# First norms turned to token partitions, short loads on SyncE's queue, gate rank in four column tiles, its logs under k and v, modulation slabs spread out

## The chip, the cores and the metric

One core of a Trainium2 chip runs the kernel. The time is device microseconds of one execution, and comparisons use the median of several. The profile is one execution. TensorE is PE in the rows (PEld its weight loads), VectorE DVE, ScalarE ACT, GpSimd POOL, SyncE SP. A q behind an engine's name is its instruction queue issuing a DMA.

## The reference

A transformer stack on 256 tokens of width 1024. The first block, cut to what matters:

```
sh1, sc1, g1, sh2, sc2, g2      = split(silu(c) @ w_mod + b_mod)        # x
csh1, csc1, ...                 = split(silu(c_ctx) @ w_mod + b_mod)    # context
hc = rmsnorm(ctx, norm1_g) * (1 + csc1) + csh1
hx = rmsnorm(x,   norm1_g) * (1 + sc1)  + sh1
u, q, k, v, g, gates, lr = split(h @ w_in)      # lr: 2 x 16 columns, "gate rank"
la_f = log_sigmoid(lr_f @ a2_f + ab_f) / 16     # the same for b; for hx and hc
pooled = centred_pool(ux) - ux
o = gla_bidirectional(qx, kx, vx, la_x, state from kc, vc, la_c)
x = x + g1 * mixer_out(pooled, o, g, gates)     # sigmoid gates, w_pool_br, w_gla_br, w_o
x = x + g2 * hier_moe(rmsnorm(x, norm2_g) * (1 + sc2) + sh2)   # 32 experts
```

Behind it come a final norm and a second block: two layers (block attention, dilated attention), each with a layer norm and an MLP of width 4096 with squared relu. The change touches the first block up to `w_o` only.

## The kernel before

**Slabs.** Weights come in slabs of 2 MB. `slab_plan()` lists them; SyncE issues them in that order (the loop over `SLAB_AT`, `load`, L592). Up to the experts a slab's number modulo 4 is its slot, so a slab can be issued only when the slab four places ahead of it in the list has been read (`slab_freed`). `w_mod` is slabs mod 0 to 11 (512 columns each); mod 0 and 1 are the shift of the first norm, 2 and 3 its scale, 4 to 11 the rows g1, sh2, sc2, g2. `w_in` slab 0 is u, 1 q, 2 k, 3 and 4 v, 5 and 6 g, 7 to 10 the gates.

**Banks.** `bank_plan()` lists every PSUM result in order with the engine that reads it out (V: VectorE, A: ScalarE). A ring of 4 banks is used in that order; `bank()` on TensorE waits until the result four places back was read out. `moved(engine, name, i)` waits for one read-out. A second PSUM area, `acc`, holds sums of w_o and later.

**Order of the work.** Each engine has one program. On TensorE: ctx and x tiles are turned so that features lie on partitions (`turn`, L1625); the small vectors are turned (L1674); for each of the two norms eight matmuls with a ones matrix sum the squares over features (`norm_sum`, L1737); four modulation row products (`mod_rows`, L1685: column tiles of 32, so four partial sums over two steps), whose rows are copied by ScalarE (L719) and turned to columns by tiny matmuls (`mod_cols`, L1692); VectorE then forms hT and cT (`affine`, L1082). The gate rank `lr` (L1754) is one 16-column product at a time for direction and stream, copied by ScalarE to `lrT` (L762); the gate product `z` (L1762) adds the bias by a 17th row of ones. ScalarE takes the absolute value (L767), exp (L769) and ln (L770), VectorE min (L1101) and the difference (L1107), which gives L, the log decay. Then cumulative sums and remainders of L (L1770, L1775, L1782, L1784) with exp on ScalarE, k for x and context (`fmajor` L1632, `tmajor` L1639), ktok, v (eight products of 32 records), q, the four heads (L1817 to L1844), u, pooling (L1857) and y1 (L1865).

After that come the exact products: `f_half` takes half a slab, split into a high part by ScalarE (`split_hi`, L735) and a low part by VectorE (`split_lo`, L1031), two halves ahead (`WB`), and makes three matmuls per block (L1644 to L1646). Between these halves stand `mod_rows(4)` to `mod_rows(11)` and the broadcasts of their rows over all partitions (`mod_bc`, L1697), the slabs taking turns in `slab_plan()`. Then the `w_o` sums (L1710 to L1712), and everything behind.

**Small loads.** ScalarE's queue issues ten short loads after x has landed (`small`, L694): the rank weights (rows of 128 B), pool weights, router weights (rows of 16 and 128 B), the gate matrices and biases. One semaphore counts all ten. SyncE issues identity, ctx, x, six vector rows, the other constants and then slabs.

## Time and profile before

| | us |
|---|---|
| time before, median of 3 (lowest to highest) | 1555.63 (1553.88 to 1557.14) |
| the profiled execution's own time | 1555.18 |
| its span | 1553.4 |
| TensorE matmul busy in the span | 1396.1 |
| VectorE busy | 652.8 |
| ScalarE busy | 467.8 |
| DMA, mean over the span | 239 GB/s |

The span runs from the first to the last instruction; times of day in the rows count from its start. Mean granted TensorE clock: 0.956 of full speed. Some rows are of one long line of work, some group many instructions.

### The profile page before, as it was taken

Reading aid. Unit: us, or ns where it says so; the run is one execution under the profiler, and the core shown is the slowest. Engines: PE = TensorE matmul, PEld = TensorE weight load, DVE = VectorE, ACT = ScalarE, POOL = GpSimd, SP = SyncE. Lnnn points to the kernel's source line nnn. Section 1 sums busy time; section 2 is a strip of 40 time slices with the busy share of each in tenths; the row PEclk is TensorE's granted clock in tenths of the full one; section 3 lists DMA queues with packets and bytes.
Section 4 is the critical chain, followed back from the end, with each engine's and each line's share of the span. In section 5 each row is a group of like instructions: output and inputs, shape, how many; then the busy total and the mean of one; then the engine's idle time right before and its main releaser. Section 6 shows DMA issues by size and latency. Waiting matters only on the chain.

```text
span 1553.4 us, 20788 instructions
## 1 busy us (share of the span) xinstructions
PE 1396.1 (90%) x8683; PEld 1005.6 (65%) x8683; DVE 652.8 (42%) x968; ACT 467.8 (30%) x598; POOL 0.2 (0%) x4
## 2 busy tenths in 40 slices
PE   3889998999969998888888969997999989799998
PEld 2445464787854443443443439987999879689997
DVE  1322033333552331231222336657555576565555
ACT  1260112341331221111111134544333345443332
POOL 0000000000000000000000000000000000000000
PEclk6889999999969999999999989998999999989999
DMA  9601221876648999999999995243554525345430
GB/s 320 217 1 54 84 106 54 310 274 247 227 163 367 427 430 427 430 427 430 427 429 428 428 405 200 106 165 121 198 217 170 209 90 182 124 163 185 155 148 27
DMA packets 88678, 371.77 MB, mean 239 GB/s; under 512 B 6356, under 2 KB 8194, under 8 KB 76196
## 3 DMA queue, kind: packets, MB, share of 16 engines
q1 hardware_dynamic: 84604, 369.40, 60.6%
q10 hardware_dynamic: 4008, 1.40, 0.4%
q8 instruction: 52, 0.85, 0.2%
q14 instruction: 14, 0.11, 0.0%
HBM read 369.74 MB, written 1.05 MB: 239 GB/s over the span
## 4 chain that ended last, share of the span: by engine, by line
PE 67%; DMA 19%; DVE 6%; ACT 5%; issue 2%; ACTq 1%; DVEq 0%; SPq 0%
DMA arena<-in_moe_w 18%; PE ring L1644 6%; PE ring L1645 6%; PE ring L1646 6%; PE ring L1639 5%; PE acc L1710 4%; PE acc L1711 4%; PE acc L1712 4%; PE ring L1966 4%; PE acc L1991 3%; PE ring L1632 3%; PE ring L1981 2%; PE acc L1644 2%; PE acc L1646 1%; PE acc L1645 1%
## 5 line engine op out<-in xcount | busy, mean ns | idle before, releaser
L859 ACT ACTIVATE arena<-ring 128x512 f32<-128x512 f32 x80 | 52.9, 661 | 382.7 <-PE ring L1966 230.0
L1031 DVE TENSOR_TENSOR wlo<-slots,whi 128x2048 fp32r<-128x2048 f32 x56 | 128.0, 2288 | 73.6 <-ACT whi L735 73.6
L1348 DVE COPY arena<-ring 128x512 f32<-128x512 f32 x48 | 44.5, 927 | 240.9 <-PE ring L1966 213.0
L735 ACT ACTIVATE whi<-slots 128x2048 fp32r<-128x2048 f32 x56 | 106.9, 1913 | 97.5 <-PE acc L1712 62.4
L1991 PE MATMUL acc<-arena 128*128 128x512 f32 x256 | 118.4, 605 | 0.0
L1966 PE MATMUL ring<-slots,arena 128*32 128x512 f32 x768 | 94.0, 618 | 13.0 <-DMA slots<-in_moe_w 13.0
L1991 PEld LDWEIGHTS acc<-arena 128*128 128x128 f32 x256 | 46.1, 190 | 73.3 <-issue 45.8
L1646 PE MATMUL ring<-xhi,wlo 128*128 128x256 f32 x320 | 90.7, 283 | 0.0
L1645 PE MATMUL ring<-xlo,whi 128*128 128x256 f32 x320 | 90.7, 283 | 0.0
L1644 PE MATMUL ring<-xhi,whi 128*128 128x256 f32 x320 | 90.6, 283 | 0.0
L1973 PEld LDWEIGHTS ring<-const,arena 128*128 128x128 f32 x512 | 63.4, 196 | 38.4 <-issue 16.7
L1031 DVE TENSOR_TENSOR w1lo<-slots,w1hi 128x2048 fp32r<-128x2048 f32 x20 | 45.8, 2292 | 89.5 <-ACT w1hi L735 89.5
L1639 PE MATMUL ring<-slots,arena 128*128 128x512 f32 x192 | 83.0, 593 | 0.0
L1973 PE MATMUL ring<-const,arena 128*128 128x128 f32 x512 | 75.0, 292 | 2.8 <-DVE arena L1348 0.6
L1644 PE MATMUL acc<-xhi,whi 128*128 128x256 f32 x224 | 67.7, 302 | 3.5 <-DVE xlo L1390 3.5
L1966 PEld LDWEIGHTS ring<-slots,arena 128*32 128x32 f32 x768 | 21.5, 111 | 73.6 <-issue 53.7
L1710 PE MATMUL acc<-whi,hidhi 128*128 128x512 f32 x176 | 69.1, 392 | 0.0
L1711 PE MATMUL acc<-wlo,hidhi 128*128 128x512 f32 x176 | 68.8, 391 | 0.0
L1712 PE MATMUL acc<-whi,hidlo 128*128 128x512 f32 x176 | 68.5, 389 | 0.0
L1639 PEld LDWEIGHTS ring<-slots,arena 128*128 128x128 f32 x192 | 36.4, 190 | 44.8 <-issue 44.8
L1646 PE MATMUL acc<-xhi,wlo 128*128 128x256 f32 x224 | 64.9, 290 | 0.0
L1645 PE MATMUL acc<-xlo,whi 128*128 128x256 f32 x224 | 64.7, 289 | 0.0
(317 smaller groups left out, 2976.0 us busy)
## 6 DMA issues: line engine op xcount, KB each, us to landing
slots<-in_moe_w SPq DMA_DIRECT2D x64, 2048.0 KB, 24.6
arena<-in_moe_w SPq DMA_DIRECT2D x32, 2048.0 KB, 27.2
slots<-in_mlp_w_in SPq DMA_DIRECT2D x16, 2048.0 KB, 9.2
slots<-in_mlp_w_out SPq DMA_DIRECT2D x16, 2048.0 KB, 7.7
slots<-in_w_mod SPq DMA_DIRECT2D x12, 2048.0 KB, 8.6
slots<-in_w_in SPq DMA_DIRECT2D x11, 2048.0 KB, 12.2
slots<-in_moba_w_qkv SPq DMA_DIRECT2D x6, 2048.0 KB, 20.1
slots<-in_dil_w_qkv SPq DMA_DIRECT2D x4, 2048.0 KB, 8.0
```

Of the source, the lines that this page charges most:

```text
L735: act.activation(hi, raw, ACT.Copy).then_inc(G["whi_ready"], 1)
L1031: dve.tensor_tensor(lo, raw, hi.bitcast(F32), ALU.subtract).then_inc(G["split_ready"], 1)
L1639: ins = pe.matmul(b[:, 0:n], x[:, kt, tt * P:(tt + 1) * P], w[:, kt, 0:n], start=(kt == 0), stop=(kt == ks - 1))
L1644: pe.matmul(o, whi_, xhi_, start=first, stop=False, skip_group_check=True)
L1645: pe.matmul(o, whi_, xlo_, start=False, stop=False, skip_group_check=True)
L1646: return pe.matmul(o, wlo_, xhi_, start=False, stop=last, skip_group_check=True)
L1710: pe.matmul(o, hi[:, k0 + k, t_], wh[:, k, c], start=(first and k == 0), stop=False, skip_group_check=True)
L1711: pe.matmul(o, hi[:, k0 + k, t_], wl[:, k, c], start=False, stop=False, skip_group_check=True)
L1712: ins = pe.matmul(o, lo[:, k0 + k, t_], wh[:, k, c], start=False, stop=(last and k == ks - 1), skip_group_check=True)
L1966: ins = pe.matmul(b[32 * g:32 * g + 32, :], xs[:, kt, j, :], w[:, kt, :], start=(kt < 4), stop=(kt >= 4))
L1973: ins = pe.matmul(b[:, f * P:(f + 1) * P], src[:, f * P:(f + 1) * P], C("fold"), start=True, stop=True)
L1991: ins = pe.matmul(acc[:, tt, f], putT[:, j, tt * P:(tt + 1) * P], ys[:, f], start=False, stop=True, skip_group_check=True)
```

## The change

The norms of ctx and x are taken with tokens on partitions: ScalarE squares a token tile and sums along the row, takes one root for each pair, VectorE scales the rows, and then the tiles are turned. Scale and shift follow in two halves of features, x on VectorE, context on ScalarE. The modulation slabs come in the order 0, 2, 1, 3. Vector rows move to ScalarE's queue; the ten short loads move to SyncE's, at four places of the slab list, with three semaphores in place of one; the gate matrices are loaded twice, to partitions 0, 32, 64 and 96. The rank's four products go to four column tiles of one bank. The gate's eight products read partitions 0, 32, 64, 96 and go to four ring banks and four banks of `acc`; exp and ln are each done for both halves in a row. The k products of x, two v products and modulation slab 4 stand between the gate and the cumulative sums. Modulation slabs 4 to 8 stand among v and q, 9 and 10 in the heads, 11 at u. `w_in` 5 to 10 follow all modulation slabs in the list. All four bias rows are broadcast at once when hT is complete.

```diff
+MODS = (0, 2, 1, 3)
 def slab_plan():
-    order = [("mod", s) for s in range(4)]
-    order += [("w_in", 2), ("w_in", 3), ("w_in", 4), ("w_in", 1), ("w_in", 0)]
-    order += [("mod", 4), ("w_in", 5), ("mod", 5), ("w_in", 6), ("mod", 6)]
-    for s in range(4):
-        order += [("w_in", 7 + s), ("mod", 7 + s)]
-    order += [("pool_br", 0), ("mod", 11), ("gla_br", 0), ("gla_br", 1), ("w_o", 0), ("w_o", 1)]
+    order = [("mod", s) for s in MODS]
+    order += [("w_in", 2), ("w_in", 3), ("mod", 4), ("mod", 5), ("w_in", 4), ("mod", 6), ("w_in", 1), ("mod", 7)]
+    order += [("mod", 8), ("w_in", 0), ("mod", 9), ("mod", 10), ("mod", 11)]
+    order += [("w_in", s) for s in range(5, 11)]
+    order += [("pool_br", 0), ("gla_br", 0), ("gla_br", 1), ("w_o", 0), ("w_o", 1)]
     order += [("moe", s) for s in range(3 * NE)]
     for l in range(2):
...
-                if (name, s) == ("w_in", 5):
-                    sp.wait_ge(G["h_ready"], 2 * KT)
-                    spread(bc_g1, a["b_mod"][0][2 * D:3 * D], bc_in)
-                    spread(bc_sh2, a["b_mod"][0][3 * D:4 * D], bc_in)
+                if (name, s) == ("w_in", 2):
+                    sp.dma_start(w_lr[:, :, :], a["w_in"][0][:, 5632:5664].rearrange("(k p) n -> p k n", p=P)).then_inc(lr_in, 16)
+                    for j in range(4):
+                        d = "fb"[j % 2]
+                        sp.dma_start(a2[32 * j:32 * j + RANK, :], a["gla_a2_" + d][0]).then_inc(lr_in, 16)
+                        sp.dma_start(a2[32 * j + RANK:32 * j + RANK + 1, :], a["gla_ab_" + d]).then_inc(lr_in, 16)
+                if (name, s) == ("w_in", 3):
+                    sp.dma_start(const[:, P + 2:], a["consts"][:, P + 2:]).then_inc(consts_in, 16)
+                if (name, s) == ("mod", 4):
+                    sp.wait_ge(G["h_ready"], KT)
+                    for j, dst in enumerate((bc_g1, bc_sh2, bc_gain2, bc_g2)):
+                        spread(dst, a["b_mod"][0][(2 + j) * D:(3 + j) * D], bc_in)
+                if (name, s) == ("mod", 6):
+                    sp.dma_start(w_pool[:, :, :], a["pool_w"][0].rearrange("g c e -> c g e")).then_inc(pool_in, 16)
+                if (name, s) == ("w_in", 0):
+                    sp.dma_start(w_rt[:, :, 0:NG], a["router_grp_w"][0].rearrange("(k p) n -> p k n", p=P)).then_inc(router_in, 16)
+                    sp.dma_start(w_rt[:, :, NG:], a["router_exp_w"][0].rearrange("(k p) n -> p k n", p=P)).then_inc(router_in, 16)
+                    sp.dma_start(rb[0:1, 0:NG], a["router_grp_b"]).then_inc(router_in, 16)
+                    sp.dma_start(rb[0:1, NG:], a["router_exp_b"]).then_inc(router_in, 16)
                 if (name, s) == ("gla_br", 1):
                     sp.wait_ge(bank_full, BANK_AT["gate", 7] + 1)
...
-            act.wait_ge(tokens_in["x"], 16)
-            small(w_lr[:, :, :], a["w_in"][0][:, 5632:5664].rearrange("(k p) n -> p k n", p=P))
-            small(w_pool[:, :, :], a["pool_w"][0].rearrange("g c e -> c g e"))
-            small(w_rt[:, :, 0:NG], a["router_grp_w"][0].rearrange("(k p) n -> p k n", p=P))
-            small(w_rt[:, :, NG:], a["router_exp_w"][0].rearrange("(k p) n -> p k n", p=P))
-            for d, name in enumerate("fb"):
-                small(a2[0:RANK, d, :], a["gla_a2_" + name][0])
-                small(a2[RANK:RANK + 1, d, :], a["gla_ab_" + name])
-            small(rb[0:1, 0:NG], a["router_grp_b"])
-            small(rb[0:1, NG:], a["router_exp_b"])
...
-                mod_rows(s)
+            act.wait_ge(G["eps_ready"], 1)
+            for n, (src, name) in enumerate(((ctok, "ctx"), (xtok, "x"))):
+                act.wait_ge(tokens_in[name], 16)
+                for tt in range(TT):
+                    i = TT * n + tt
+                    act.activation(squares[i], src[:, tt, :], ACT.Square, accum_out=nss[:, i:i + 1]).then_inc(G["square_ready"], 1)
+                act.wait_ge(G["square_ready"], TT * n + TT)
+                pair = slice(TT * n, TT * n + TT)
+                act.activation(nstd[:, pair], nss[:, pair], ACT.Sqrt, bias=oeps[:, 0:1], scale=1.0 / D).then_inc(G["nstd_ready"], 1)
+            for i in range(4):
+                tt, q = divmod(i, 2)
+                b = take("c_tiles", i).rearrange("p (k t) -> p k t", k=4)
+                act.activation(cT[:, 4 * q:4 * q + 4, tt * P:(tt + 1) * P], b, ACT.Copy).then_inc(freed["A"], 1)
+            def c_affine(q):
+                act.wait_ge(G["mod_ready"], q + 1)
+                for kt in range(4 * q, 4 * q + 4):
+                    act.activation(cT[:, kt, :], cT[:, kt, :], ACT.Identity, bias=mod[:, kt, 1:2], scale=scale1[:, 1, kt:kt + 1]).then_inc(G["c_ready"], 1)
+            moved(act, "c_tiles", 3)
+            mod_rows(0)
+            mod_rows(2)
+            mod_rows(1)
+            c_affine(0)
+            mod_rows(3)
+            c_affine(1)
+            b = take("lr", 0)
             act.wait_ge(G["lr_ones"], 1)
-            for i in range(2):
-                b = take("lr", i)
-                ins = act.activation(lrT[0:RANK, 2 * i:2 * i + 2, :], b[0:RANK, :].rearrange("p (d t) -> p d t", d=2), ACT.Copy)
-                ins.then_inc(freed["A"], 1)
+            for j in (2, 3):
+                p_ = slice(32 * j, 32 * j + RANK)
+                act.activation(lrT[p_, :], b[p_, 0:T], ACT.Copy).then_inc(G["lr_part"], 1)
+            for tt in range(TT):
+                for j in range(4):
+                    if tt == 0:
...
+                if i == 0:
+                    mod_rows(11)
                 split_hi(i)
             for i in range(4):
-                if i % 2 == 0:
-                    mod_rows(4 + i // 2)
                 b = take("g", i)
                 split_hi(i + WB)
                 ins = act.activation(gT[:, 2 * i:2 * i + 2, :], b.rearrange("p (k t) -> p k t", k=2), ACT.Silu)
...
+            for n, src in enumerate((ctok, xtok)):
+                dve.wait_ge(G["nstd_ready"], n + 1)
+                pair = slice(TT * n, TT * n + TT)
+                link(dve.reciprocal(nstd[:, pair], nstd[:, pair]))
+                for tt in range(TT):
+                    dve.tensor_scalar(src[:, tt, :], src[:, tt, :], nstd[:, TT * n + tt:TT * n + tt + 1], None, ALU.mult).then_inc(G["tn_ready"], 1)
+            for i in range(4):
+                tt, q = divmod(i, 2)
+                b = take("x_tiles", i).rearrange("p (k t) -> p k t", k=4)
+                dve.tensor_copy(xT[:, 4 * q:4 * q + 4, tt * P:(tt + 1) * P], b).then_inc(freed["V"], 1)
+            for q in range(2):
+                mod_cols(q)
+                mod_cols(2 + q)
+                moved(dve, "mod_cols", 2 + q)
+                v = slice(4 * q, 4 * q + 4)
+                for r in range(2):
+                    ins = dve.scalar_tensor_tensor(scale1[:, r, v], mod[:, KT + 4 * q:KT + 4 * q + 4, r], 1.0, col("norm1_g", 4 * q, 4), ALU.add, ALU.mult)
+                ins.then_inc(G["mod_ready"], 1)
+                moved(dve, "x_tiles", 3)
+                dve.wait_ge(G["mod_ready"], q + 1)
+                for kt in range(4 * q, 4 * q + 4):
+                    dve.tensor_scalar(hT[:, kt, :], xT[:, kt, :], scale1[:, 0, kt:kt + 1], mod[:, kt, 0:1], ALU.mult, ALU.add).then_inc(G["h_ready"], 1)
+            b = take("lr", 0)
+            for j in range(2):
+                p_ = slice(32 * j, 32 * j + RANK)
+                if j == 1:
+                    dve.wait_ge(G["lr_part"], 2)
+                ins = dve.tensor_copy(lrT[p_, :], b[p_, 0:T])
+            ins.then_inc(freed["V"], 1)
+            for tt in range(TT):
+                for j in range(4):
+                    dve.wait_ge(G["abs_ready"], 4 * tt + j + 1)
+                    dve.tensor_scalar(L[:, 2 * j + tt, :], z_bank(j, tt), 0.0, None, ALU.min).then_inc(freed["V"] if tt == 0 else v_step, 1)
+                    n_step[0] += tt
+            for i in range(2):
+                ins = dve.tensor_copy(kT[:, 2 * i:2 * i + 2, :], take("kT", i).rearrange("p (h t) -> p h t", h=2))
...
+            split_lo(0)
+            mod_bc(11)
+            split_lo(1)
             for i in range(2):
                 ins = dve.tensor_copy(pooled[:, 2 * i:2 * i + 2, :], take("pool", i).rearrange("p (g t) -> p g t", g=2))
...
-            def norm_sum(name, k, src):
-                b = bank(name, k)
-                for kt in range(KT):
-                    ins = pe.matmul(b[:, 0:T], ones, src[:, kt, :], start=(kt == 0), stop=(kt == KT - 1))
-                full(ins)
-            for k in range(2):
-                pe.wait_ge(G["sq_ready"], k + 1)
-                norm_sum("norm", k, sq)
-            for s in range(4):
+            for n, s in enumerate(MODS):
                 mod_rows(s)
-                if s:
...
+            mod_cols(MODS[-1])
+            pe.wait_ge(lr_in, 16 * 9)
+            b = bank("lr", 0)
+            for kt in range(KT):
+                pe.wait_ge(G["h_ready"], kt + 1)
+                pe.wait_ge(G["c_ready"], kt + 1)
+                for j in range(4):
+                    d = j % 2
+                    ins = pe.matmul(b[32 * j:32 * j + RANK, 0:T], w_lr[:, kt, d * RANK:(d + 1) * RANK], (hT, cT)[j // 2][:, kt, :],
+                                    start=(kt == 0), stop=(kt == KT - 1))
+            full(ins)
+            moved(pe, "lr", 0)
+            for tt in range(TT):
+                for j in range(4):
+                    p_ = slice(32 * j, 32 * j + RANK + 1)
+                    o = bank("z", j) if tt == 0 else z_bank(j, tt)
+                    pe.matmul(o, lrT[p_, tt * P:(tt + 1) * P], a2[p_, :], start=True, stop=True).then_inc(bank_full if tt == 0 else G["z2_ready"], 1)
+            wk = arrive("w_in", 2, KT, 512)
+            for i in range(2):
+                full(fmajor(bank("kT", i), wk, hT, 2 * i * P, 2))
+            mod_rows(4)
+            def values_x_or_c(i):
+                s, j = divmod(i, 4)
+                w = arrive("w_in", 3 + s, KT, 512)
+                full(tmajor(bank("v", i), w, (hT, cT)[j // 2], j % 2))
+            values_x_or_c(0)
+            pe.wait_ge(consts_in, 16)
+            mod_bc(4)
+            values_x_or_c(1)
             for i in range(4):
                 d, hp = divmod(i, 2)
                 pe.wait_ge(G["L_ready"], d + 1)
...
                                             S[:, d, n, :], start=False, stop=(d == 1), skip_group_check=True)
                 full(ins)
+                if h > 1:
+                    mod_bc(h + 7)
+                if 0 < h < 3:
+                    mod_rows(h + 8)
             w = arrive("w_in", 0, KT, 512)
-            for i in range(2):
-                ins = tmajor(bank("u", i), w, hT, i)
-                full(ins)
+            full(tmajor(bank("u", 0), w, hT, 0))
+            mod_rows(11)
+            full(tmajor(bank("u", 1), w, hT, 1))
+            mod_bc(11)
             moved(pe, "u", 1)
             for i in range(2):
                 b = bank("pool", i)
```

## Rows read from the trace of the kernel before

**Rows 1.** Chain of waits, 340 to 441 us: start, length, what ran or was awaited.
```profile
341.39 0.86 PE ring L1697 x2
...
365.23 0.59 ACT arena L819
...
414.13 0.47 PE acc L1710
```

**Rows 2.** Chain of waits, 0 to 110 us.
```profile
1.65 7.27 DMA arena<-in_x
...
13.26 6.54 ACTq L694
...
19.83 5.84 ACTq L694
...
58.66 1.89 PE ring L1692 x16
...
61.62 15.67 PE ring L1754 x64
...
95.20 1.91 ACT arena L770
```

**Rows 3.** Groups by shape on TensorE, 0 to 260 us: count, busy us, mean ns, idle.
```profile
L1754 PE MATMUL ring<-arena 128*16 128x256 f32 x64 | 15.7, 411 | 1.1 <-DVE arena L1082 1.1
...
L1685 PE MATMUL ring<-slots,arena 128*32 128x512 f32 x64 | 7.5, 597 | 0.0
```

**Rows 4.** Windows: length, busy by engine, then clock, DMA share, GB/s.
```profile
15.00:30.00 15.00, 0.31 (x1) 0.18 (x1) 0.07 (x1) 2.44 (x4) 0.00 (x0) 0.50 1.10 354
...
55.00:60.00 5.00, 5.00 (x45) 2.79 (x37) 0.88 (x4) 1.19 (x2) 0.00 (x0) 1.00 1.05 397
...
82.90:96.60 13.70, 8.15 (x24) 4.93 (x23) 4.93 (x7) 13.60 (x12) 0.00 (x0) 0.51 0.00 1
...
270.00:274.00 4.00, 4.00 (x21) 1.32 (x19) 1.75 (x4) 0.00 (x0) 0.00 (x0) 0.57 0.07 22
...
434.50:455.00 20.50, 16.01 (x57) 12.80 (x58) 9.06 (x27) 8.69 (x11) 0.00 (x0) 0.51 0.44 187
```

**Rows 5.** Groups by shape on ScalarE, 0 to 260 us.
```profile
L767 ACT ACTIVATE arena<-ring 128x512 f32<-128x512 f32 x8 | 4.4, 595 | 2.0 <-PE ring L1762 2.0
...
L769 ACT ACTIVATE arena<-arena 128x2048 f32<-128x2048 f32 x2 | 3.8, 1910 | 0.0
...
L802 ACT ACTIVATE arena<-arena 128x256 f32<-128x256 f32 x8 | 3.3, 416 | 0.2
...
L769 ACT ACT_TABLE_LOAD x2 | 2.6, 1283 | 0.0
```

**Rows 6.** Chain of waits, 0 to 340 us, its part from 108 us.
```profile
108.78 13.81 PE ring L1632 x64
...
137.20 54.93 PE ring L1639 x128
...
207.53 1.97 PE ring L1817 x8
...
249.08 13.95 PE ring L1639 x32
```

**Rows 7.** DMAs: ScalarE's queue, 0 to 400 us; landing of w_in slabs, 0 to 350.
```profile
q10 hardware_dynamic: 3720, 0.61, 1.0%
...
DMA to landing us min/median/max: 7.9/12.2/18.2
```

**Rows 8.** Timeline in order of time, 249 to 310 us.
```profile
263.04 0.37 SPq L592 DMA_DIRECT2D slots<-in_w_in  x1
...
265.47 2.29 DVE L1031 TENSOR_TENSOR w1lo<-slots,w1hi 128x2048 fp32r<-128x2048 f32 x1 [4.58 <-ACT w1hi L735]
...
269.01 2.55 PE L1865 MATMUL ring<-arena 128*128 128x256 f32 x8 [3.27 <-DVE arena L1169]
...
274.43 0.38 PE L1644 MATMUL ring<-hhi,w1hi 128*128 128x256 f32 x1
```

More of the change, by code:

```diff
@@ L269, in build @@
         sq = at(20 * K1, KT, T)
+        squares = [at(o * K1, D) for o in (20, 21, 24, 25)]
         cT = at(22 * K1, KT, T)
@@ L1130, in _ @@
                 ins.then_inc(freed["V"], 1)
+            for s in range(5, 8):
+                mod_bc(s)
             for i in range(2):
@@ L1696, in mod_bc @@
                 moved(pe, "mod_rows", s)
-                full(pe.matmul(bank("mod_bc", s), C("selb"), mod_row[:, s % 2, :], start=True, stop=True))
+                full(pe.matmul(bank("mod_bc", s), C("selb"), mod_slot(s), start=True, stop=True))
             def t_half(h, hi, lo, k0, first, last, f0, tiles=(0, 1), ready=None):
@@ L1757, in _ @@
-            moved(pe, "lr", 1)
-            for i in range(8):
-                st, tt = divmod(i, 2)
-                d = st % 2
-                b = bank("z", i)
-                full(pe.matmul(b, lrT[:, st, tt * P:(tt + 1) * P], a2[:, d, :], start=True, stop=True))
+            for n, s in enumerate(MODS):
+                mod_rows(s)
+                if n:
+                    mod_cols(MODS[n - 1])
+            mod_cols(MODS[-1])
+            pe.wait_ge(lr_in, 16 * 9)
+            b = bank("lr", 0)
@@ L1785, in _ @@
                 full(ins)
-            w = arrive("w_in", 2, KT, 512)
             for i in range(2):
-                full(fmajor(bank("kT", i), w, hT, 2 * i * P, 2))
-            for i in range(2):
-                ins = tmajor(bank("kc", i), w, cT, i)
-                full(ins)
+                full(tmajor(bank("kc", i), wk, cT, i))
             moved(pe, "kT", 1)
@@ L1877, in _ @@
                 turn("oT", i, otok, *divmod(i, 2))
[L1878 to L1885 removed]
+            for i in range(8):
+                f_half(bank("gate", i), 4 + i, hhi, hlo)
             w = arrive("pool_br", 0, POOLG, D)
```

293 lines of the change are left out of this document (109 added, 184 removed).

## Prediction

> **What bounds the kernel now.** I read the chain of waits first, then windows of busy time with the granted clock, then groups by shape on TensorE and ScalarE, then the SyncE issues. From 0 to the first sum matmul of w_o at 414.1 us [rows 1] the chain is never held by the slab stream as a whole: it is a string of waits on one core's program order. From there on (experts, both attention layers, both MLPs, about 1139 us) the change touches no instruction, and the expert stage starts from the end of w_o; so whatever w_o gains or loses I carry to the end one for one.
>
> Before 414 us there are four places to see. (1) Up to 60.6 us, where the last modulation columns end [rows 2]: x lands at 8.9, then ScalarE's queue issues ten short loads until 27.5, two of them holding it 6.54 and 5.84 us, and both norms run one after the other through TensorE. (2) 61.6 to 77.3: the gate rank, 15.67 us of TensorE on 16 columns [rows 2, 3]. (3) 77.3 to 99.6: gate and its logs; from 82.9 to 96.6 ScalarE works 13.6 of 13.7 us while TensorE's clock is granted at 0.51 [rows 4], that is mostly the 1.2 GHz level. (4) From 271 to 414 TensorE is full, with eight modulation slabs between the large products.
>
> **The change part by part.** Each step gets its new time of day; durations are those of before.
>
> *Start.* The slabs of modulation 0, 2, 1, 3 now set the pace. Ahead of the last of them lie the identity and pair columns, ctx, x and four slabs: 0.07 + 2.10 + 8.39 = 10.55 MB. With the short loads beside them the DMAs moved 354 GB/s, without them 397 [rows 4]. I take 380 and 2.5 us before bytes flow: 30.3 us (354 to 397 gives 29.1 to 32.3). The norms are ready before that: the rows load on ScalarE's queue, two pairs of squares, two roots and four scalings by row (1 to 1.3 us each at these lengths), and eight transposed tiles, end near 23 even if half of them run at the low clock. Then row product 3 (1.87 us, a fourth of the group at L1685 [rows 3]), its copy behind four context affines on ScalarE (0.42 us each [rows 5]), column products 1 and 3: 34.6 us where it was 60.6. Gain 26.
>
> *Gate rank.* 32 matmuls of 256 columns now go to four column tiles. L1685 is the row for that: 16 records of 512 columns in 1.87 us, 0.117 each, where a 512-column record alone takes 0.43 (13.81 us for 64 of half that length [rows 6]). So 64 records of 256 columns take 64 x 0.058 = 3.7 us. Bounds: 3.7, and 15.7 if the tiles did not overlap. I take 3.7, since L1685 has the same K, type and tile width. End 38.3. The copies are now two on ScalarE and, after them, the last on VectorE, 1.4 us instead of 0.6: 39.7.
>
> *Gate.* Eight matmuls with 17 rows, now at partitions 0, 32, 64, 96. No row of before shows four row tiles at once; one after the other they take two 0.43 us records each (6.9 in all), overlapped four deep two rounds of 0.86 and a start, 1.9. The Trainium skill, TensorEngine Tiling (Array Packing), Performance Considerations, says a contract dimension up to 32 tiles fourfold; by it 1.9, and no row here shows that. I take 1.9 because the bank destinations are separate, and keep 6.9: 41.6 us. The two kT products (13.8 [rows 6]) then run beside the logs. The logs need 8 x 0.55 + 4 x 1.91 + 2 x 1.28 = 14.6 us [rows 5] (two table loads instead of four), so they end near 55, and four subtractions of 1.2 us on VectorE near 59; nobody waits, since the cumulative sums come at 73. This cover is worth the 19 us of logs and waits between 77.9 and 97.1 [rows 2].
>
> *Modulation 4 arrives late.* SyncE waits for all of hT (36.5 us), then issues four broadcasts of bias rows (2.1 MB) and slab 4. From 30.3 the queue holds the short rows, w_in 2, the constants 1.25 MB, w_in 3, the broadcasts, slab 4: 9.6 MB at 380 is 25.3 us, plus the short rows. ScalarE's queue moved 3720 packets in 1.0% of 400 us [rows 7], so 1100 packets cost 1.2 us: slab 4 is in at 57. kT ends at 55.4; TensorE waits 1.6 us. This wait also swallows the first 1.6 us of any slower gate or rank.
> The Trainium skill, DMA: Bandwidth & Descriptors, Specifications, speaks against the move: transfers under 512 B per row fall off line rate. Our rank weights are 128 B rows and stand in front of w_in 2 in one queue; the row on the 3720 packets says this costs about a microsecond.
>
> *k, v, q with modulation 4 to 8.* Row product 4, v0, broadcast 4 (0.86 [rows 1]), v1: 57 to 73.5. Sums and remainders 12.2 (14.4 in the trace, part of it at the low clock), kc 13.7, ktok 0.9: 100.3. Then six v tiles (54.93 for eight [rows 6]) 41.2, qT 13.8, four row products 7.4, four broadcasts 3.4. Slab 6 is freed only by v3, slab 8 by v7; each has one product (6.9 and 7.8) in front of it against the shortest landing of 7.9 [rows 7]: 1.1 + 0.3 us. Heads start at 168.2; they started at 207.5.
>
> *Heads and u.* 41.5 us as before [rows 6], plus row products 9, 10 and 11 (5.6), broadcasts 9 and 10 (1.7) and 1 us for their handovers, plus u (13.9): u ends at 232.0 (before 263.0).
>
> *A new wait.* w_in 5 sat in its slot 60 us early; now its slot is the one u reads, so it is issued at the end of u and lands 7.9 us later. ScalarE's order is split 0, then the copy of u1; TensorE's pooling waits for that copy. Chain: landing 7.9, split 1.9, copy 0.6; pooling 2.0 while ScalarE splits 1; VectorE low half 0, broadcast 11, low half 1, pooled copies (2.3 + 0.7 + 2.3 + 1.3): 16.5; y1 2.6: first gate matmul at u + 19.2 = 251.2. Before it was at u + 11.4, with 2.9 of row product 4 inside [rows 8]. During the wait of 10 us TensorE's clock falls (0.57 after a lesser one [rows 4]); I add 2.5 us of half speed in pooling and the first g half.
>
> *Large products.* 274.4 to 414.1 [rows 1, 8] less seven row products (13.0), eight broadcasts (6.9), and the 1.7 us that ypool waited for a gate [rows 1] behind the late gla_br slab: 139.7 - 21.6 = 118.1. w_o starts at 251.2 + 2.5 + 118.1 = 371.8, before 414.1: 42.3 us earlier. The splits (1.9 and 2.3 us for each half) stay under the 5.8 us of a half.
>
> The profiled execution took 1555.2 us (span 1553.4 and 1.8 around it), 0.4 below the median. 1555.2 - 42.3 = 1512.9; I say **1513 us**.
>
> **Rivals.**
> *Tiles don't overlap.* Rank +12.0, gate +5.0, less the 1.6 us that slab 4 swallows: 1513 + 15.4 = 1528 with both, 1516.4 with the gate alone. For: no row tiles in the trace. Against: L1685.
> *Short rows clog SyncE.* Each of the rank's weight loads as slow as the two that held ScalarE's queue, 6.54 + 5.84: 12.4 us before lr and w_in 2, 1525. For: the queue did stall there. Against: those stalls happened with the engines full of slabs (354 GB/s went on flowing), so they are back pressure.
> *The clock stays low after the new wait.* From 434.5 to 455 it stayed at 0.51 for 20.5 us though TensorE was busy 16.0 of them [rows 4]. The same after u: 20 us at half speed give back 10 instead of 2.5: 1520.5. Against: there the matmuls were small and halting.
> *The new wait is shorter than I think, or the early phase finishes sooner* (slab 4 on time, faster slabs): 3 to 8 us better, 1507.
> *Slower than before.* One mechanism: TensorE stays at 1.2 GHz from the gate through v, q and heads because it never gets going. From 57 to 232 it has about 150 us of matmuls that run at the high clock in the trace; at half speed they double, 150 us more, 1663. It decides from 42 us of matmul at the low clock on. Against: after each pause in the trace the high clock came back within some 7 us of dense matmuls, and v is dense.
>
> **How the numbers follow.** Forecast 62%, with a range of its own of 1507 to 1519; tiles 10% (most of it the gate alone), clog 6%, clock after u 10%, better than forecast 8%, slower 2%; 2% for no change at all, in case a stage behind w_o takes back all. The range 1504 to 1526 takes in the likeliest, the clock, the clog and the better case and the lesser tile case. A measurement of this kernel tells 0.2% (3.1 us) from nothing. Faster 0.96, same 0.02, slower 0.02.
>
> **What would show it.** In the new profile: last modulation column near 34.6; the rank group four times shorter; gate records short or 0.86 apart; TensorE dense from 42 us but for a gap near 55; heads from 168; u ending at 232; then a gap of about 10 us on TensorE with w_in 5 landing inside it; no row products after 235; w_o from 372. Wrong if slab 3 lands after 33, if v or q wait on slabs for more than 3 us in all, or if the gap behind u is over 15.

## The result, and the profile after

The changed kernel takes **1520.4 us** (median of four runs, 1519.04 to 1522.69). The kernel before took 1555.47 us beside it (four runs, 1553.88 to 1557.14). The ratio is 0.9776, with a 95% interval of 0.9759 to 0.9793: faster by 35 us. The forecast was 1513 us, so it is 7.4 us too low: inside the whole range of 1504 to 1526, but 1.4 us outside the range of 1507 to 1519 that the likeliest case had for itself. The profiled execution took 1521.46 us, with a span of 1519.7 us at a granted clock of 0.960 (before 0.956).

The chain of waits of the changed kernel, 0 to 441 us (start, length, what ran or was awaited):

```profile
10.78 21.47 DMA slots<-in_w_mod
...
32.30 3.37 PE ring L1696 x16
...
37.54 3.62 PE ring L1757 x64
...
45.09 15.74 PE ring L1646 x64
...
77.47 3.57 PE ring L1788 x32
...
121.05 8.02 DMA slots<-in_w_mod
...
154.77 8.43 DMA slots<-in_w_mod
...
237.25 7.93 DMA slots<-in_w_in
...
245.21 1.92 ACT w1hi L733
...
247.15 2.29 DVE w1lo L1053
...
249.44 0.60 DVE arena L1079
250.04 2.20 DVE w1lo L1053
252.24 1.21 DVE arena L1192 x2
253.49 3.77 PE ring L1893 x8
...
378.96 0.47 PE acc L1721
```

Read it beside [rows 1, 2, 6]. The start is now one long wait for a modulation slab (10.78 to 32.30). The rank group is 3.62 us long, where it was 15.67. No ScalarE log stands in the chain between the gate and the sums. The big gap of before between the last modulation column and k has gone, and a new one has opened at 237.25: from the end of u to the first gate matmul at 257.3, TensorE's order hangs on the landing of w_in 5 and then on five short steps of ScalarE and VectorE. On this chain w_o comes in at 378.96 instead of 414.13, 35.2 us earlier. These are the sum matmuls that wait for the last part of their input; the first ones, which the prediction took 414.1 for, ran at 406.62 before and run at 371.02 now, 35.6 us earlier. Behind 378.96 the span has 1140.7 us left, where it had 1139.3 behind 414.13.

Windows of the changed kernel (length, busy by engine, clock, DMA share, GB/s):

```profile
3.00:28.00 25.00, 13.24 (x97) 8.79 (x97) 6.02 (x12) 11.60 (x20) 0.00 (x0) 1.00 1.04 388
28.00:32.00 4.00, 0.25 (x3) 0.16 (x2) 1.78 (x7) 2.07 (x4) 0.00 (x0) 0.98 1.12 303
32.00:37.00 5.00, 4.71 (x29) 2.00 (x29) 0.17 (x1) 0.60 (x1) 0.00 (x0) 0.67 1.05 379
46.00:50.00 4.00, 4.00 (x13) 3.21 (x13) 3.12 (x6) 3.97 (x6) 0.00 (x0) 0.64 1.03 406
237.00:257.30 20.30, 8.67 (x29) 6.77 (x28) 7.17 (x7) 4.19 (x3) 0.00 (x0) 0.66 0.87 311
257.30:271.00 13.70, 13.70 (x116) 13.70 (x115) 3.33 (x4) 5.90 (x5) 0.00 (x0) 1.00 0.93 329
```

Two things are to be seen. In the last four microseconds before slab 3 is in, TensorE is idle and the DMAs move 303 GB/s, not 388. And around the pauses of TensorE the clock falls: it is granted at half from 31.9 to 35.3 us, that is from just before the end of the wait for slab 3, and again from 45.5 to 48.9 us and inside the new gap, so that the windows there show about 0.65. Once the gate's products run dense it is 1.00 again.

Groups by shape on TensorE, 0 to 260 us, of the changed kernel:

```profile
L1765 PE MATMUL ring<-arena 17*128 17x512 f32 x8 | 1.1, 640 | 1.3 <-DVE arena L1110 1.3
L1765 PE MATMUL acc<-arena 17*128 17x512 f32 x8 | 1.0, 587 | 0.0
```

Sixteen gate records with a mean of about 600 ns are done in 2.1 us of busy time: they lie four deep over each other. In the trace they start in fours, at 42.5, 43.0, 43.4 and 43.9 us.

### The profile page after: what moved, and what is told of

Its sections match the earlier page's. It is cut to its first block, busy times and chain, and to the rows that moved or that the text cites. A ratio compares the mean times of both kernels' runs of the same rounds, so it can differ in the third digit from the quotient of the medians.

```text
span 1519.7 us, 20742 instructions
## 1 busy us (share of the span) xinstructions
PE 1372.5 (90%) x8651; PEld 994.1 (65%) x8651; DVE 645.3 (42%) x966; ACT 467.0 (31%) x608; POOL 0.2 (0%) x4
## 4 chain that ended last, share of the span: by engine, by line
PE 66%; DMA 21%; DVE 6%; ACT 4%; issue 2%; SPq 1%; DVEq 0%; ACTq 0%
DMA arena<-in_moe_w 18%; PE ring L1658 6%; PE ring L1659 6%; PE ring L1660 6%; PE ring L1653 5%; PE acc L1721 4%; PE acc L1722 4%; PE acc L1723 4%; PE ring L1979 4%; PE acc L2004 3%; DMA slots<-in_w_mod 2%; PE ring L1646 2%; PE ring L1994 2%; PE acc L1658 2%; PE acc L1659 2%
## 5 line engine op out<-in xcount | busy, mean ns | idle before, releaser
L733 ACT ACTIVATE w1hi<-slots 128x2048 fp32r<-128x2048 f32 x20 | 38.2, 1910 | 91.3 <-PE ring L1660 71.2
```

What stands on the lines that cost most here:

```text
L733: act.activation(hi, raw, ACT.Copy).then_inc(G["whi_ready"], 1)
```

## Experiments

The first six undo or repair one part each, the next three go into the start, the last are combinations. All ratios are against the kernel before, and "w_o" is the time of the first sum matmul of w_o in the profiled execution, which is 371.02 us in the changed kernel. Of the expectations, the one on the slabs that are not spread (365 and 379) counts w_o on the chain of waits, 8 us later; the others that name 371, 363, 357 or 354 count it as here.

### The gap behind u: copies before the low halves

```diff
@@ ScalarE, end of u
                 if i == 0:
                     mod_rows(11)
+            for i in range(2):
                 split_hi(i)
@@ VectorE
-            split_lo(0)
             mod_bc(11)
-            split_lo(1)
             ... pooled and y1 copies ...
+            split_lo(0)
+            split_lo(1)
```

> The changed kernel, with the copy of u1 on ScalarE ahead of the first two high halves, and the pooling and y1 copies on VectorE ahead of the first two low halves. Theory (the gap behind u is one chain: landing of w_in 5 7.9, high half 1.9, and only then the copies that pooling and y1 wait for): pooling and y1 run while w_in 5 lands, the first gate matmul comes 12.2 us behind u instead of 20.0, and the time falls by 8 us to about 1512.5. Rival (the slab's landing alone makes the gap, so the order of copies is free): first gate matmul still 18 to 20 us behind u, time unchanged at 1520.4.

Measured 1517.49 us (1516.09 to 1520.11), ratio 0.9754 [0.9734, 0.9775]. Its chain of waits:

```profile
238.06 8.12 DMA slots<-in_w_in
...
246.21 1.92 ACT w1hi L733
...
248.15 2.30 DVE w1lo L1054
...
250.59 0.55 PE ring L1659
```

The gate's product starts 12.5 us after u instead of 20.0: the pooling chain has left the path and only landing, one high and one low half stand in it. So the gap is made as the prediction said, and 7.5 us of it are a matter of order. w_o starts 5.7 us earlier, but the median moved by only 2.9 us where 8 were expected. In the profiled execution the expert stage behind w_o took 460.7 us (419.85 to 880.56) instead of 458.1 (425.53 to 883.66); 1.6 us of that is longer TensorE time (411.21 instead of 409.64 us busy), at a mean clock of 0.97 instead of 0.98. That stage has no instruction of the edit in it, and no run shows why it differs.

### w_in 5 fetched before u

```diff
-    order += [("mod", 8), ("w_in", 0), ("mod", 9), ("mod", 10), ("mod", 11)]
-    order += [("w_in", s) for s in range(5, 11)]
+    order += [("mod", 8), ("w_in", 0), ("mod", 9), ("mod", 10), ("w_in", 5), ("mod", 11)]
+    order += [("w_in", s) for s in range(6, 11)]
...
-    order += [("u", 0, "A"), ("mod_rows", 11, "A"), ("u", 1, "A"), ("mod_bc", 11, "V")]
+    order += [("u", 0, "A"), ("u", 1, "A")]
...
+    order += [("g", 0, "A"), ("mod_rows", 11, "A"), ("g", 1, "A"), ("mod_bc", 11, "V"), ...]
```

> The changed kernel, with w_in 5 ahead of modulation 11 in the slab list, so that its slot comes free at q; row product and broadcast 11 behind the first and second g half. Theory (the gap behind u is made by the slot that w_in 5 shares with u's slab): no slab wait behind u, first gate matmul about 9 us behind u instead of 20.0, no low clock there, time about 1508 (12 us less). Rival (w_in 5 early collides with the loads of modulation 9 and 10 and of the heads, or modulation 11 is now late): the gap moves behind the first g half and the time falls by less than 4 us.

Measured 1513.12 us (1508.24 to 1515.57), ratio 0.9717 [0.9694, 0.9741], 7.3 us under the changed kernel, where 12 were expected. u ends at 238.27; its chain of waits goes on:

```profile
238.27 0.60 ACT arena L833
...
244.24 1.99 PE ring L1892 x8
```

No landing stands in it. The gate's product starts at 245.88, 7.6 us after u. w_o comes 8.0 us earlier, although in this execution the clock was low from 30.8 to 44.4 us and the early phase ended later for it.

### The modulation slabs where they were

The order of slabs, products and broadcasts 4 to 11 is put back as in the kernel before (slabs among w_in 5 to 10 and behind them, products between the gate's halves); everything else stays.

```diff
-    order += [("w_in", 2), ("w_in", 3), ("mod", 4), ("mod", 5), ("w_in", 4), ("mod", 6), ...]
+    order += [("w_in", 2), ("w_in", 3), ("w_in", 4), ("w_in", 1), ("w_in", 0)]
+    order += [("mod", 4), ("w_in", 5), ("mod", 5), ("w_in", 6), ("mod", 6)]
+    for s in range(4):
+        order += [("w_in", 7 + s), ("mod", 7 + s)]
```

> The changed kernel, with the slab list from w_in 2 on, and the row products and broadcasts of modulation 4 to 11, back where they were in the kernel before; everything else of the change stays. Theory (spreading them moves TensorE work without removing any, and its waits cost): the gap behind u shrinks from 20.0 to 11.4 us with row product 4 inside, the waits on slabs 6 and 8 (1.2 and 0.7 us), the handovers in the heads (1) and the wait of 3.3 us at the turned heads go, 1.7 us at ypool come back; w_o starts near 365 instead of 379, time 1506 to 1508. Rival (the spreading is part of the gain, since the large products no longer wait for slabs): w_o starts later than 379 and the time is 1522 to 1542.

Measured 1513.98 us (1509.23 to 1514.39), ratio 0.9733 [0.9717, 0.9749]: **6.4 us faster than the changed kernel**, though 6 us slower than expected. The profiled execution, the fastest of the four, has this in its chain of waits:

```profile
198.79 13.95 PE ring L1649 x32
...
213.35 1.81 ACT w1hi L734
...
222.50 2.83 PE ring L1692 x16
...
225.34 0.32 PE ring L1654
```

u ends at 212.75, the high half of w_in 5 is split straight away, and the gate's product follows 12.6 us after u, with a row product in it. The heads, too, start at 157.25 and not at 173.86, since four row products and their broadcasts no longer stand before them. w_o comes 12.2 us earlier in this execution; by the medians 6.4 us are left of it, and why the other executions are 4 to 5 us slower than this one is open. Moving the slabs was thus a loss of some 6 us inside a change that wins 35.

### The gate rank tile by tile

```diff
-            for kt in range(KT):
-                pe.wait_ge(G["h_ready"], kt + 1)
-                pe.wait_ge(G["c_ready"], kt + 1)
-                for j in range(4):
-                    d = j % 2
+            pe.wait_ge(G["h_ready"], KT)
+            pe.wait_ge(G["c_ready"], KT)
+            for j in range(4):
+                d = j % 2
+                for kt in range(KT):
```

> The changed kernel, with the rank's 32 matmuls ordered tile by tile (eight of one column tile in a row) instead of one of each tile in turn. Theory (the shortening comes from overlap of four neighbouring column tiles): the rank group takes about 14 to 15.7 us instead of 3.65, gate and all behind it 11 to 12 us later, time 1531 to 1532. Rival (the engine orders tiles by itself, or the shortening is from the 16-column form): the group stays near 4 us and the time at 1520.4.

Measured 1537.84 us (1534.45 to 1537.98), ratio 0.9879 [0.9859, 0.9899]: 17.4 us slower than the changed kernel. The chain of waits:

```profile
36.52 3.52 PE ring L1703 x16
...
42.75 14.07 PE ring L1757 x63
```

The windows of that group, these matmuls alone (TensorE, its weight loads, then clock, DMA share, GB/s):

```profile
42.75:48.15 5.40, 5.40 (x14) 1.86 (x16) 0.50 1.05 398
48.15:56.82 8.67, 8.66 (x52) 3.80 (x48) 1.00 1.04 394
```

The same 32 matmuls (64 records in the trace), into the same four column tiles, take 14.07 us when the eight of one tile follow each other, and 3.6 when neighbours go to different tiles. But the first 5.4 us of the 14.07 ran at half clock, and the 3.6 did not. Records of one tile start 0.427 us apart at the low clock and 0.216 us apart at the high one; only where one tile's row ends and the next begins do a few of them overlap. My estimate for the group at the high clock throughout is 14.07 - 2.7 = 11.4 us, so the order itself costs some 7.7 us. Of the 17.4 us the rest is the low clock in the group (2.7), my edit waiting for all features before its first matmul (2.7), and last columns that end 2.5 us later, since in this execution the clock was low from 31.1 to 48.1 us and slab 3 was used 0.6 us later. Some 2 us stay without a cause.

### The sums before k and v

The products of k, modulation 4 and the first two v tiles are moved behind the cumulative sums on TensorE, ScalarE and VectorE, so nothing covers the logs.

```diff
+            # cumulative sums and remainders here
             wk = arrive("w_in", 2, KT, 512)
             for i in range(2):
                 full(fmajor(bank("kT", i), wk, hT, 2 * i * P, 2))
             mod_rows(4)
             values_x_or_c(0)
             mod_bc(4)
             values_x_or_c(1)
-            # cumulative sums and remainders here
```

> The changed kernel, with k, row product 4, v0, v1 and broadcast 4 placed behind the cumulative sums again, so that nothing covers the logs. Theory (the cover is worth what the logs take on ScalarE less nothing): TensorE idles from 44.5 us until L of the first direction is ready near 57, 12.5 us, and 1 to 3 us of low clock follow; time 1533 to 1536. Rival (the wait for slab 4 and the later slab waits absorb the delay): slab 4's landing is reached in both, time 1520 to 1526.

Measured 1531.98 us (1531.74 to 1538.22), ratio 0.9847 [0.9831, 0.9864]: 11.6 us slower. The chain of waits, in the slowest of its executions:

```profile
48.54 4.01 ACT arena L777 x8
...
62.24 5.47 PE ring L1775 x32
```

TensorE waits from the gate's end at 49.9 to 62.24, 12.3 us, and the chain is ScalarE's absolute values, exp and ln with their table loads.

### Short loads back on ScalarE's queue

```diff
@@ SyncE, in front of w_in 2 (mod 6 and w_in 0: the pool and router loads)
-                    sp.dma_start(w_lr[:, :, :], a["w_in"][0][:, 5632:5664]...)
-                    for j in range(4):
-                        ... gla_a2, gla_ab ...
@@ ScalarE, before the norms
+            act.wait_ge(tokens_in["x"], 16)
+            act.dma_start(w_lr[:, :, :], a["w_in"][0][:, 5632:5664]...)
+            ... pool_w, router, gla_a2, gla_ab ...
```

> The changed kernel, with all the short loads back on ScalarE's queue behind the arrival of x (four pairs for the gate now, so 14 loads). Theory (their issue holds ScalarE some 18 us, with silu, squares and roots behind it): the norms' tiles come near 38 instead of 19.7, the last column near 46, time 1528 to 1531. Rival (the slabs are the bound and hide it): last column stays within 2 us of 37.5, time 1519 to 1522.

Measured 1536.09 us (1533.92 to 1537.08), ratio 0.9868 [0.9851, 0.9884]: 15.7 us slower. The chain of waits:

```profile
9.09 0.41 ACTq L705
...
12.90 6.63 ACTq L708
...
19.56 5.90 ACTq L711
...
34.83 5.84 PE ring L1639 x32
...
52.23 5.31 PE ring L1757 x64
```

ScalarE stands in the issues until 28.4 us, as in [rows 2], before it squares anything; the tiles are turned from 34.83 to 40.66 instead of 14.05 to 19.7, and the last column ends at 52.2 instead of 37.5. That is 6 us behind the expectation, and so the time is 5 us over it: the tiles are 2.7 us later than the 38 expected, and the four row products, their columns and ScalarE's context affines between them take 11.5 us behind the tiles, not 8. The two issues of 6.63 and 5.90 us are those of [rows 2] again, and in both cases the DMAs were full of slabs while they lasted, which fits back pressure on the issuing engine. They are the loads of router weights (rows of 128 B) and of the first gate matrix (16 rows of 2 KB). The rank weights, rows of 128 B too, were issued in 0.41 us (L705), so it is not the short rows that make an issue long. SyncE in the changed kernel, in order of time, says the same: the first gate matrix is issued in 3.75 us and its second copy in 0.31, and four slabs of 2 MB take 13.92.

```profile
2.16 13.92 SPq L605 DMA_DIRECT2D slots<-in_w_mod  x4
16.12 5.29 SPq L629 DMA_DIRECT2D arena<-in_w_in  x1
21.46 3.75 SPq L632 DMA_DIRECT2D arena<-in_gla_a_f  x1
...
27.79 0.31 SPq L632 DMA_DIRECT2D arena<-in_gla_a_f  x1
```

### Half of two slabs

Slabs 1 and 3 are fetched only by half; half of the sums of these two modulations are left out.

```diff
+                if SLABS[n] in (("mod", 1), ("mod", 3)):
+                    sp.dma_start(view(...)[:, 0:4, :], src[:, 0:4, :]).then_inc(landed[SLOT_OF[n]], 16)
+                    return
...
-                for half in range(2):
+                halves = 1 if s in (1, 3) else 2
+                for half in range(halves):
```

> The changed kernel, loading and using only the first half (features 0 to 511) of modulation slabs 1 and 3; the rest of their sums is left out. Theory (the landing of the fourth slab sets the start): slab 3 lands 5.4 us earlier, the last modulation column comes at 32 instead of 37.5, less 0.9 us more for each half product; time 1513 to 1515. Rival (the norms or the chain of tiles set the start): last column not before 36, time 1519 to 1521.

Measured 1514.55 us (1514.1 to 1517.23), ratio 0.9736 [0.972, 0.9753], 5.9 us faster. TensorE in order of time:

```profile
26.22 1.06 PE L1700 MATMUL ring<-slots,arena 128*32 128x512 f32 x8
...
29.41 1.87 PE L1707 MATMUL ring<-const,arena 128*128 128x2 f32 x8 [1.14 <-ACT arena L721]
```

The last column is done at 31.2 instead of 37.5 and w_o starts 6.4 us earlier: in the changed kernel the start is bound by the slabs' bytes, and what is won there reaches the end nearly one for one (6.3 us at the last column, 5.9 in the time). Here TensorE works without a pause from 19.7 to 28.3 us, so its own chain of products has become the bound; that still fewer bytes would win nothing more is argued from this and not shown.

### TensorE kept busy before slab 3

```diff
+                if n == 3:
+                    for _ in range(4):
+                        pe.matmul(acc[:, 0, 0:512], ident, xtok[:, 0, 0:512], start=True, stop=True)
```

> The changed kernel with four extra matmuls (512 columns, 3.4 us together, into an unused bank) on TensorE while it waits for modulation slab 3. Theory (the short wait drops the granted clock, and row product 3 and the first part of kT pay for it): row product 3 takes 1.9 instead of 3.4 us, kT 13.8 instead of 15.7, w_o starts 1.5 to 3.4 us earlier, time 1517 to 1519. Rival (the clock falls for another reason): row product 3 stays at 3.4 us, time 1520 to 1521.

The four matmuls write a bank that nobody reads then. Measured 1518.76 us (1517.56 to 1521.67), ratio 0.9763 [0.9747, 0.978]: 1.6 us under the changed kernel, within the intervals. TensorE in order of time:

```profile
31.73 1.92 PE L1696 MATMUL ring<-slots,arena 128*32 128x512 f32 x16
```

The row product takes 1.92 us instead of 3.37, so its length was the clock's doing. The columns end at 35.5. But the clock fell later, from 42.2 to 49.1 us, behind the pauses at rank and gate: part of what was won was given back in kT, and w_o starts 1.9 us earlier.

### Rank loads one slab later

```diff
-                if (name, s) == ("w_in", 2):
+                if (name, s) == ("w_in", 3):
                     sp.dma_start(w_lr[:, :, :], ...)
```

> The changed kernel, with the rank's nine loads issued behind w_in 2, before the constants, instead of in front of it. Theory (short rows run beside the last bytes of slab 3, where the DMAs moved 303 instead of 387 GB/s, and delay its landing by about 1 us): slab 3 is used at 31.3 instead of 32.3, but the rank then waits for its weights until about 39, so gate is 1 to 2 us later and the time 1520 to 1523. Rival (the short rows cost nothing, the start is bound by the slabs' bytes alone): row product 3 starts at 32.3 again.

Measured 1521.72 us (1520.28 to 1521.82), ratio 0.978 [0.9765, 0.9795]: no gain. One line of its windows, and two pieces of its chain of waits:

```profile
28.00:32.00 4.00, 0.47 (x7) 0.39 (x11) 1.78 (x7) 2.07 (x4) 0.00 (x0) 1.00 1.05 385
```

```profile
25.32 8.46 SPq L632
...
38.77 5.38 PE ring L1756 x64
```

Without the short rows the DMAs move 385 GB/s in the last four microseconds, not 303, but slab 3 is used only 0.45 us sooner (31.85). That is less than executions differ: the ten that have the short rows in front of w_in 2 and fetch slab 3 whole use it between 31.8 and 33.0 us. So this run can't say that they delay it at all. The issues themselves then become the wait: that of the first gate matrix, 16 rows of 2 KB, holds SyncE for 8.46 us, the last of the nine loads lands at 38.7, and the rank starts 1.2 us later than in the changed kernel, at the low clock.

### Combinations

Three kernels put the repairs together. The first is w_in 5 early with the four matmuls before slab 3. The second is the same with the turned heads behind the first gate half. The third is the old slab order with the four matmuls.

> As the run with w_in 5 early, plus four extra matmuls before row product 3. Theory (low clock at slab 3 costs it the 4 us by which its kT came later than in the changed kernel, 49.6 against 45.1): last column near 35.5, kT from 43, w_o near 357 instead of 363, time 1507 to 1511. Rival (no gain from the clock): 1513.

> The changed kernel with three edits together: w_in 5 ahead of modulation 11 (as in the run with w_in 5 early), four extra matmuls before row product 3, and the turned heads behind the first gate half. Theory (the three losses are separate: the slot behind u 9 to 12, the low clock at slab 3 2, the wait of 3.3 us at the turned heads): w_o starts near 354 where the changed kernel had 371, time 1503 to 1507, and TensorE has no wait over 1 us between the turned heads and the second gate half. Rival (the expert stage is bound by its own slab stream, whose start doesn't move with TensorE): time stays at 1512 to 1514 as with w_in 5 early alone.

> The run with the slabs not spread, plus the four extra matmuls before row product 3. Theory (where the modulation products stand is worth nothing by itself; only the slab waits are): it ties with the run that keeps them spread with w_in 5 early and the extra matmuls, 1506 to 1511, ratio 0.969 to 0.972. Rival (spread products are worth what they take out of the large products, once w_in 5 is early): 3 us or more slower than that run, 1511 or more.

| kernel | median us (range) | ratio [95%] |
|---|---|---|
| w_in 5 early, TensorE busy | 1508.21 (1506.96 to 1513.34) | 0.9707 [0.9689, 0.9724] |
| the same, turned heads later | 1508.05 (1504.31 to 1511.01) | 0.9695 [0.9679, 0.9711] |
| old slab order, TensorE busy | 1507.86 (1507.42 to 1509.1) | 0.9699 [0.9686, 0.9713] |

All three beat both kernels, by some 12 us the changed one, and can't be told from each other. The second has a new wait in its chain:

```profile
275.63 1.91 ACT w1hi L733
277.56 1.28 ACT L846
```

The turned heads now wait 2.7 us on ScalarE's high half and a table load, where the two waits around them were 3.3 us, so moving them gave next to nothing; w_o comes at 357.16 instead of 354, and the time misses the expected 1503 to 1507. That the first and the third tie says that the place of the row products is itself worth nothing that these runs can tell: what costs is the slab that lands late because of it.

The four matmuls are worth more here than in the changed kernel: 4.9 us with w_in 5 early (1513.12 to 1508.21) and 6.1 us in the old slab order (1513.98 to 1507.86), against 1.6. In the profiled execution of the first kernel the clock did not fall before 239 us, in that of the second it was low from 42.1 to 49.0 us. What decides between the two is not shown. With the four matmuls in both, spreading the slabs costs 10.9 us (1518.76 against 1507.86) and not 6.4.

## Why the prediction was nearly right, step by step

The mechanisms were right and the sizes of several terms off; at w_o they add up to 7.2 us (378.96 against 371.8), and the stages behind it add 1.4 (1140.7 against 1139.3).

- **Start: 34.6 forecast, 37.5 measured.** The tiles were ready at 19.7 (forecast 23) and hid behind the slabs, as said. Slab 3 was used at 32.30, not 30.3. The 380 GB/s held to 28 us (388); the last four microseconds ran at 303. The term that was short is the bytes: up to 32.30 us the DMAs had moved 11.15 MB (345 GB/s over the whole stretch), and the sum stops at 10.55. So 0.6 MB that the sum put behind slab 3 moved before it could be used, which is my estimate of 1.6 us at its 380 GB/s. Why they went first no run shows, and the run that moved the short rows does not tell their part from the spread between executions. Most of the rest, 1.5 us, is row product 3 at 3.37 instead of 1.87: I counted TensorE's wait for the slab but not what it does to the clock. The run that kept TensorE busy shows it (1.92). The start was worth 23 us of the 26.
- **Gate rank 3.7: measured 3.6.** Undoing the interleaving brings back 14.07, or an estimated 11.4 at the high clock. The tile width and K of the row product group were the right row to read.
- **Gate 1.9: measured 2.1 of busy time.** Four row tiles overlap, which no row of before showed. The Trainium skill, TensorEngine Tiling (Array Packing), Performance Considerations, gives row tiling by four for a contract dimension of 32; the products of 17 rows agree with it here. The tile rival (10%) is out.
- **kT 41.6 to 55.4, then a wait of 1.6 for slab 4: measured 45.09 to 60.83, no wait.** The two products took 15.74 and not 13.8, since the clock stood at half from 45.5 to 48.9 us. The delay ate the wait that I had foreseen, so the step came out 3.8 late and not 5.4.
- **Logs under k and v: held.** With the subtractions they end at 66.1 (forecast 59), the sums come at 77.47, nobody waits. Without the cover it costs 11.6 us measured.
- **Short loads on SyncE: held.** The clog rival (6%) is out for this order: the issues took 5.29 and 3.75 us on SyncE, but nothing behind them was late. The run that moved them behind another slab shows what that rival would have looked like: 8.46 us of one issue, in front of the rank. The rival took its price from the two long issues of before, but these were router weights and a gate matrix; the rank weights were issued there in 0.43 us, and in 5.29 us on SyncE. What makes an issue long is thus not the length of its rows. The Trainium skill, DMA: Bandwidth & Descriptors, Specifications, warns of transfers under 512 B. With the short rows beside the last bytes of slab 3 the DMAs moved 303 GB/s, without them 385, which fits it; but slab 3 came at most about 1 us later for it (31.85 us without them, 31.8 to 33.0 with them). What cost time was the order of the issues, and the measurement decides.
- **Slabs 6 and 8, 1.1 and 0.3: measured 1.15 and 0.65.** The landings were 8.02 and 8.43 us. The heads start at 173.86 (forecast 168.2): 4.1 carried from kT and the products up to ktok, 0.7 on the way through q, and 0.9 in the handover from q to the heads: I let it take 0.7, it takes 1.56.
- **Heads and u: 63.8 forecast (168.2 to 232.0), 63.4 measured.**
- **The new wait: u + 19.2 and 2.5 for the clock, measured u + 20.0 in all, 1.7 less.** Landing 7.93 (7.9), split 1.92 (1.9), pooled copies 1.21 (1.3), y1 3.77 at the low clock (2.6). Two runs shortened it: to 12.5 by order alone, to 7.6 by the earlier slab. The clock-stays-low rival (10%) is out: it was 1.00 from 257.3 to 284 us.
- **Large products 118.1: measured 121.7.** The ypool wait went, as said. In its place TensorE waits at the turned heads, where a row product used to fill the time; this was the one wait that I had not foreseen.

Waits of TensorE in the changed kernel, 257 to 380 us (us in total, times, longest):

```profile
PE ring L1658 <- DVE arena L1208: 2.0, 1, 2.0
...
PE ring L1639 <- ACT arena L841: 1.3, 1, 1.3
```

These are 3.3 us, where the same stretch of before had 0.8 of small waits that are gone. Behind them the clock stood at 0.55 from 285 to 292, over 6.5 us of matmuls, which is about 3 us more; before, it was 1.00 in every window of this stretch. The whole stretch, before and after:

```profile
274.43:414.13 139.70, 135.26 (x1005) 116.57 (x1001) 57.73 (x50) 47.42 (x44) 0.00 (x0) 1.00 0.77 277
257.30:378.96 121.66, 116.42 (x872) 112.63 (x871) 53.88 (x44) 43.32 (x36) 0.00 (x0) 0.97 0.52 188
```

New waits of 2.5 us and some 3 us of low clock would be 5.5 to 6, and the miss is 3.6. So the row products and broadcasts that left the stretch were worth some 2 us more than the 19.9 that I took off: the busy time fell by 18.8 us, and by about 22 if the low clock is taken out. No row says why.

Where the 35 us come from is then read from the runs that undo one part each, in microseconds against the changed kernel: rank tiles 17.4 (some 7.7 of it the order of the tiles themselves), short loads 15.7, logs under k and v 11.6, slabs spread out -6.4. The turned norms were not undone alone; the tiles were ready 12.6 us before slab 3 was, and three row products with their columns stand between, 7.4 us of them in the run with the loads on ScalarE (40.66 to 48.06), so a norm path slower by up to some 5 us should have cost nothing with the loads on SyncE; that is argued and not shown. The parts need not add up, since each undone one is measured with the others in place.

Two errors happened to work against the others, and that is luck: the wait of 1.6 us for slab 4 did not come, because TensorE was late for it, and the new gap was 1.7 us shorter than forecast. Without them the forecast would have been some 3 us further off. Of the three signs of being wrong none showed: slab 3 was used at 32.3 (limit 33), v and q waited 1.8 us on slabs (limit 3), and TensorE was idle for 11.7 us behind u (limit 15).

What stays open: why the DMAs moved less in the last microseconds before slab 3, and why the stages behind w_o, from its first sum matmul on, take between 1146.8 and 1151.7 us in kernels that are identical there.

## What to carry to other kernels

When a slab order is changed, list for each slab which product frees its slot and what stands between that and its own first use: the one that had been early for nothing (w_in 5) is the one that now costs 8 us of landing and a chain of small copies. Where TensorE waits for something, price the work right behind the wait at the low clock too. And undo the parts one at a time even when the whole is a win: one of these five was a loss.

## What the runs showed of the hardware

- Four row tiles of 17 rows at partitions 0, 32, 64 and 96, each into banks of its own, overlap: eight fp32 products of 512 columns took 2.1 us of busy time, and 6.9 would be their sum one after the other.
- Column tiles overlap only if neighbouring matmuls are in different tiles: 32 matmuls took 3.6 us in turn and 14.07 us tile by tile, 5.4 us of them at half clock (some 11.4 us at the high clock, by my estimate).
- Some issues hold their engine for microseconds while slabs are in flight: 6.63 and 5.90 us on ScalarE, 5.29 and 3.75 us or 8.46 us on SyncE. They are not the ones with short rows alone: the rank weights (128 B rows) took 0.41 us on ScalarE and 5.29 on SyncE, and one gate matrix of 16 rows of 2 KB took 3.75, 5.90 or 8.46 us, its second copy 0.31.
- In a pause of about 4 us of TensorE (28.3 to 32.3) the clock fell to half; how long that lasted differed between executions and kernels with the same start: 31.9 to 35.3 us in the changed kernel, 30.8 to 44.4 us in the one with w_in 5 early, 31.1 to 48.1 us in the one with the rank tile by tile. The executions of the kernel with w_in 5 early lie 7.3 us apart (1508.24 to 1515.57), those of the changed one 3.7.
